# Hybrid decoder trunk: the first down block moved ahead of the second gate block in the pair stream

## The chip, the cores and the metric

One core of one Trainium2 chip. The metric is device time in microseconds (us) of one execution. Three runs of the kernel before gave 1495.41, 1496.53 and 1497.82 us, so its median is 1496.53 us. Besides TensorE (PE), VectorE (DVE), ScalarE (ACT) and GpSimd (POOL), SyncE (SP) matters here, since it issues every weight transfer.

## The reference, cut to what matters

Two layers on 256 tokens of width 1024, all in float32. Layer 0 is a state-space mixer and a dense SwiGLU, layer 1 is stick-breaking attention and a routed SwiGLU with 8 experts of width 3584, of which each token takes two. Only this last part is touched:

```python
def swiglu(h, w_gate_up, w_down):
    gate, up = jnp.split(h @ w_gate_up, 2, axis=-1)
    return (jax.nn.silu(gate) * up) @ w_down
# routed: logits -> softmax -> top 2 of 8, renormalised
for e in range(N_EXPERTS):
    out = out + gates[:, e:e+1] * swiglu(tok, w_gate_up[e], w_down[e])
```

Each expert has 1024 x 7168 gate and up weights and 3584 x 1024 down weights, 44 MB, so the eight experts are 352 MB that have to come from HBM.

## The kernel before, in words

**Weights.** Every large weight comes as a granule of 2 MB (2048 KB) into a ring of seven slots (`ring`, RING = 7). A granule has a place n in one long stream; it goes to slot n % 7. SP issues the loads strictly in the order of the stream (`load`, line 511): before load n it waits until PE has released the granule seven places earlier (semaphore `used[n % 7]`), and consumers wait on `landed[n % 7]`. One SP instruction order thus governs everything: a load whose slot is already free still stands behind an earlier load whose slot is not.

**Experts.** An expert's hidden width of 3584 is cut into seven blocks f = 0..6 of 512 columns. Each block has three granules: gate (g), up (u) and down (d). The experts are taken in four pairs: expert a with many tokens, expert b with few. A pair has 42 granules, named ag, au, ad, bg, bu, bd with the block number. `pair_order` (line 74) gives their order in the stream; `PAIR_AT` and `pair_place` turn it into places, which SP, PE, ACT and DVE all use. The first five granules of the first pair (AHEAD = 5) are loaded before the routing is known, from expert 0.

**What PE does in a pair (`pair_wide`).** In block f it takes: for the tail tokens of a (up to 32 beyond 128) the product with au f, then the main product with ag f, then bg f-1, the tail's ad f, the main product with au f, bu f-1, a turn (transposes, line 2799) of the product, the tail's ag f+1, bd f-2, and last the main product with ad f. A main product splits each operand in a rounded part and a rest and runs three passes: 24 matmuls of line 2355 for one granule. Its last matmul releases the slot. ACT rounds each half granule (line 1063, `w`, a buffer of three halves) and DVE computes the rest (line 1918, `ring_lo`); both go through the granules in the order ag, au, ad of each block. Products for b and for the tail are those of line 2667 (gate and up) and line 2679 (down); they read the ring directly. In block 0 there are no b granules yet: the order of last uses is ag0, au0, ad0, ag1, bg0, au1, bu0, ad1. Before the main product of ad0 PE makes the gather of expert b's tokens (line 2622) and the turn.

**What runs.** In this trace pairs 0 and 1 have a tail (their PE rows hold tail products), pair 2 has none, and pair 3 is the light kind (`pair_light`), in which expert a has at most 64 tokens and goes through lines 2667 and 2679 too. Between pairs stand the gather for the next pair (line 2602) and the scatter of results (lines 2649 to 2659).

**The other branch.** If the routing does not allow pairs, experts run one by one with granule numbers of their own (`gate_at`, `up_at`, `down_at`). The five preloaded granules lie where the pair stream put them, so this branch has to find them there.

Of the kernel before, what the change touches and what calls it, by code (L numbers as in the profile page):

```python
# [72 lines left out]

def pair_order():

    order = [("ag", 0), ("au", 0), ("ag", 1), ("au", 1), ("ad", 0), ("bg", 0), ("ad", 1), ("bu", 0), ("ag", 2)]
    for f in range(2, FB):
        order += [("au", f), ("bg", f - 1), ("ad", f), ("bu", f - 1)]
        if f < FB - 1:
            order += [("ag", f + 1)]  # L80
        order += [("bd", f - 2)]
    return order + [("bg", FB - 1), ("bu", FB - 1), ("bd", FB - 2), ("bd", FB - 1)]
# [30 lines left out]
def pair_place(what, f):  # L113

    return N_MOE + PAIR_AT[(what, f)]


def pair_turn(p, what, f):
# [19 lines left out]
def program(nc, x, c, ada_w, ada_b, norm_g, s5_w_in, s5_lambda_re, s5_lambda_im, s5_b_re, s5_b_im,  # L138
# [3 lines left out]
    with ctx:  # L142
# [364 lines left out]
        def _(sp):  # L507
# [77 lines left out]
                for p in range(PAIRS):  # L585
                    pair_weights(p, 0 if p else AHEAD)
            with sp.Else():
                swiglu_weights(moe_w_gate_up[0][0], moe_w_down[0][0], lambda g: N_MOE + g,
                               lambda g: (N_MOE + g) // RING, AHEAD)
                with sp.Fori(1, NE) as e:  # L590
                    expert = sp.value_load(turn_i[0:1, bass.ds(e, 1)], min_val=0, max_val=NE - 1)
                    swiglu_weights(gate_up[bass.ds(expert * D, D), :], downs[bass.ds(expert * FF, FF), :],
                                   lambda g: N_MOE + g, lambda g: e * (PER_EXPERT // RING) + (N_MOE + g) // RING)
            for tt in range(TT):
                sp.wait_ge(x_new, 7 + tt)
                sp.dma_start(out[0][P * tt:P * tt + P, :], x_sb[:, tt, :]).then_inc(out_written, 16)
# [77 lines left out]
        def _(act):  # L674
# [473 lines left out]
            with act.Else():  # L1148
                with nc.Fori(0, NE, engines=[act.engine], hint_back_edge=True) as e:
# [10 lines left out]
                    def narrow(passes):  # L1160

                        if len(passes) == 2:
                            act.wait_ge(xe1_ps, e + 1)
                            for k in range(KD):
                                ins = act.activation(xe1[:, k, :], ps[:, G_BANK + k // 4, P * (k % 4):P * (k % 4) + P],
                                                     ACT.Identity, bias=shift_col(3, k), scale=scale_c[:, 3, k:k + 1])
                            ins.then_inc(xe1_done, 1)

                        def silu_item(f, ch, width):
                            if ch:  # L1170
                                act.wait_ge(t_gate, tails + f + 1)
                                if f:
                                    act.wait_ge(m_act, e * FB + f)
                                act.activation(sg[:, 0:4 * width], ps[:, G_BANK, 0:4 * width], ACT.Silu).then_inc(t_silu, 1)
                            else:
                                wait_used(act, N_MOE + gate_at(f), moe_turn(gate_at(f)))
                                if len(passes) == 2:
                                    act.wait_ge(t_act, tails + f + 1)
                                elif f:
                                    act.wait_ge(m_act, e * FB + f)  # L1180
                                act.activation(sg[:, 0:4 * width], ps[:, G_BANK, 0:4 * width], ACT.Silu).then_inc(m_silu, 1)

                        def turned_item(f, ch, width):
                            shares = P // width
                            if ch:
                                act.wait_ge(t_tr, tails + f + 1)
                            else:
                                act.wait_ge(m_tr, e * FB + f + 1)
                            src = ps[:, T_BANK, 0:4 * width].rearrange("p (c r n) -> p r c n", r=shares, n=width)
                            dst = aT[:, ch].rearrange("p (r c) n -> p r c n", r=shares)[:, :, :, 0:width]  # L1190
                            act.activation(dst, src, ACT.Copy).then_inc(t_aT if ch else m_aT, 1)

                        for f in range(FB + 1):
                            for ch, width in passes:
                                if f < FB:
                                    silu_item(f, ch, width)
                                if f:
                                    turned_item(f - 1, ch, width)
                        gathered_out(e + 1, len(passes) == 1)
                        results_out([ch for ch, _ in passes])  # L1200

                    def whole(tail):
# [3 lines left out]
                        def w_round(h):  # L1206

                            g, half = divmod(h, 2)
                            if g in plain and not half:
                                return  # L1210
                            wait_landed(act, N_MOE + g, moe_turn(g))
                            if h >= 3:
                                before, part = divmod(h - 3, 2)
                                if part:
                                    wait_used(act, N_MOE + before, moe_turn(before))
                                else:
                                    act.wait_ge(h0_read, split * PER_EXPERT + before + 1)
                            act.activation(half3(h).bitcast(F32R), ff_half(gran(N_MOE + g), half), ACT.Copy
                                           ).then_inc(whi_done, 2 if g in plain else 1)

                        def silu_main(f):
                            wait_used(act, N_MOE + gate_at(f), moe_turn(gate_at(f)))
                            if f:
                                act.wait_ge(m_act, e * FB + f)
                            act.activation(sg[:, :], ps[:, G_BANK, :], ACT.Silu).then_inc(m_silu, 1)
# [51 lines left out]
        def _(dve):  # L1277
# [714 lines left out]
            with dve.Else():  # L1992
                with nc.Fori(0, NE, engines=[dve.engine], hint_back_edge=True) as e:
# [27 lines left out]
                    def narrow(passes):  # L2021
# [6 lines left out]
                        def product_item(f, ch, width):  # L2028
# [6 lines left out]
                                                  ALU.mult).then_inc(t_act, 1)  # L2035
                            else:
                                dve.wait_ge(m_silu, e * FB + f + 1)
                                wait_used(dve, N_MOE + up_at(f), moe_turn(up_at(f)))
                                if f:
                                    dve.wait_ge(m_tr, e * FB + f)  # L2040
                                dve.tensor_tensor(a_sb[:, 0:4 * width], sg[:, 0:4 * width], ps[:, U_BANK, 0:4 * width],
# [9 lines left out]
                    def whole(tail):  # L2051
# [6 lines left out]
                        def w_rest(h):  # L2058

                            g, half = divmod(h, 2)  # L2060
                            if g in plain and not half:
                                return
                            dve.wait_ge(whi_done, (split + 1) * (2 * PER_EXPERT) + h + 1)
                            if tail:
                                dve.wait_ge(*tail_read[g])
                            dve.tensor_tensor(ff_half(ring_lo[(N_MOE + g) % RING][:, :], half).bitcast(F32R),
                                              ff_half(gran(N_MOE + g), half), half3(h), ALU.subtract
                                              ).then_inc(wlo_done, 2 if g in plain else 1)

                        def product_main(f):  # L2070
                            dve.wait_ge(m_silu, e * FB + f + 1)
                            wait_used(dve, N_MOE + up_at(f), moe_turn(up_at(f)))
                            if f:
                                dve.wait_ge(m_tr, e * FB + f)
                            dve.tensor_tensor(a_sb, sg, ps[:, U_BANK, :], ALU.mult).then_inc(m_act, 1)
# [62 lines left out]
        def _(pe):  # L2138
# [761 lines left out]
            with pe.Else():  # L2900
                scatter(0, 1)
                with nc.Fori(0, NE, engines=[pe.engine], hint_back_edge=True) as e:
# [12 lines left out]
                    def narrow(passes):  # L2915
# [32 lines left out]
                                pe.wait_ge(done_m, e * FB + f)  # L2948

                        def gate_product(f, ch, width):  # L2950
                            n = N_MOE + gate_at(f)
                            wait_landed(pe, n, moe_turn(gate_at(f)))
                            wait_last(m_silu, t_silu, f, ch)
                            product(G_BANK, ch, gran8(n), width).then_inc(t_gate if ch else used[n % RING], 1)

                        def up_product(f, ch, width):
                            n = N_MOE + up_at(f)
                            wait_landed(pe, n, moe_turn(up_at(f)))
                            wait_last(m_act, t_act, f, ch)
                            product(U_BANK, ch, gran8(n), width).then_inc(t_up if ch else used[n % RING], 1)  # L2960
# [19 lines left out]
                            ins.then_inc(t_tr if ch else m_tr, 1)  # L2980

                        def down_product(f, ch, width):
                            n = N_MOE + down_at(f)
                            wait_landed(pe, n, moe_turn(down_at(f)))
                            if ch:
                                pe.wait_ge(t_aT, tails + f + 1)
# [27 lines left out]
                    def whole(tail):  # L3014
# [3 lines left out]

                        def tail_in(g, f, at, done):

                            n = N_MOE + g
                            wait_landed(pe, n, moe_turn(g))
                            if at == TAIL_UP:
                                pe.wait_ge(t_silu, tails + f + 1)
# [8 lines left out]

                        def tail_down(g, f):

                            n = N_MOE + g
                            wait_landed(pe, n, moe_turn(g))
                            pe.wait_ge(t_aT, tails + f + 1)
                            if f == 0:
# [9 lines left out]
                            pe.wait_ge(wlo_done, (split + 1) * (2 * PER_EXPERT) + 2 * g + half + 1)  # L3049

                        def halves(g, half, cols):
                            low = ff_half(ring_lo[(N_MOE + g) % RING][:, :], half)
                            return [w.rearrange("p (k n) -> p k n", n=cols) for w in (half3(2 * g + half), low)]

                        def main_in(g, f, bank, free):

                            n = N_MOE + g
                            if f:
                                pe.wait_ge(free, e * FB + f)
                            for half in range(2):  # L3060
# [17 lines left out]

                        def main_down(g, f):

                            n = N_MOE + g
                            pe.wait_ge(m_aT, e * FB + f + 1)
                            if f == 0:
                                pe.wait_ge(sc_done, 4 * e + 8)
# [81 lines left out]
```

## Time and profile before

| | us |
|---|---|
| median of 3 runs | 1496.53 |
| the profiled execution's own time | 1497.91 |
| its span in the trace | 1496.1 |
| PE busy | 1346.0 (90%) |
| DVE busy | 673.5 (45%) |
| ACT busy | 520.2 (35%) |
| mean granted TensorE clock | 0.966 |
| weight queue's share of the 16 DMA engines' span | 81.2% |

The page cuts the span into 40 slices of 37.4 us. The routed part begins near 596 us, when the routing result lets SP and PE go on, and fills the rest. A slice's DMA digit and its GB/s say how busy the transfers were; a slice's PE digit says the same of matmuls, with the reservation that matmuls are pipelined and their ends modelled. Where both are high in the same slices, only the waits say which of the two the other one waits for.

### The profile page before, as it was taken

How to read it: one execution, taken by the hardware profiler on the slowest of the kernel's cores; microseconds unless marked ns; L12 is line 12 of the kernel's file. 1: busy time of each engine (PE TensorE's matmuls, PEld its weight loads, DVE VectorE, ACT ScalarE, POOL GpSimd, SP SyncE). 2: the span in 40 equal slices, each digit the busy share in tenths (PEclk: the TensorE clock that was granted, in tenths of full speed). 3: DMA queues.
4: the chain of work that ended last, by engine and by line, in shares of the span. 5: the costliest groups of instructions: out<-in, count | busy, mean ns of one | idle time of the engine just before them, and what ended most of it. 6: DMA issues, size and time to landing. Idle time of an engine off the chain costs nothing.

```text
span 1496.1 us, 25369 instructions
## 1 busy us (share of the span) xinstructions
PE 1346.0 (90%) x11187; PEld 966.0 (65%) x11188; DVE 673.5 (45%) x754; ACT 520.2 (35%) x566; POOL 35.8 (2%) x66
## 2 busy tenths in 40 slices
PE   3899899999999897999999999999888889887776
PEld 2674578888789646777776777766675665443332
DVE  5953344445354526655453755443764553100002
ACT  2323433343253604444442454443553442000001
POOL 3000000000010002000000000000000000000000
PEclk8989999999999997999999999999998999999999
DMA  8874794554495214689999989999999999999994
GB/s 285 323 289 156 285 394 170 203 189 169 169 340 205 75 57 171 224 337 410 412 411 412 384 319 411 411 410 412 399 351 411 414 411 411 412 412 413 412 413 190
DMA packets 206791, 474.28 MB, mean 317 GB/s; under 512 B 9986, under 2 KB 10030, under 8 KB 206670
## 3 DMA queue, kind: packets, MB, share of 16 engines
q1 hardware_dynamic: 199968, 470.83, 81.2%
q10 hardware_dynamic: 6702, 1.71, 0.5%
q8 instruction: 92, 1.51, 0.4%
q14 instruction: 29, 0.24, 0.0%
HBM read 471.47 MB, written 1.05 MB: 316 GB/s over the span
## 4 chain that ended last, share of the span: by engine, by line
PE 64%; DMA 16%; SPq 12%; DVE 3%; ACT 2%; issue 1%; ACTq 1%; POOL 0%; POOLq 0%; DVEq 0%
PE ps L2355 39%; DMA ring<-in_moe_w_down_dram 13%; SPq L511 12%; PE ps L2667 6%; PE ps L2679 5%; DMA ring<-in_ada_w_dram 3%; PE ps L2528 2%; PE ps L2331 2%; PE ps L2166 1%; PE ps L2230 1%; PE ps L2291 1%; PE ps L2622 0%; PE ps L2659 0%; PE ps L2252 0%; PE ps L2456 0%
## 5 line engine op out<-in xcount | busy, mean ns | idle before, releaser
L1918 DVE TENSOR_TENSOR ring_lo<-ring,w 128x2048 fp32r<-128x2048 f32 x126 | 288.2, 2290 | 186.3 <-ACT w L1063 149.0
L1063 ACT ACTIVATE w<-ring 128x2048 fp32r<-128x2048 f32 x126 | 240.4, 1912 | 221.0 <-PE ps L2355 208.8
L2667 PE MATMUL ps<-ring,arena 128*32 128x128 f32 (+1 forms) x5376 | 240.2, 294 | 28.6 <-DMA ring<-in_moe_w_gate_up_dram 24.8
L2667 PEld LDWEIGHTS ps<-ring,arena 128*32 128x32 f32 (+1 forms) x5376 | 183.3, 115 | 89.2 <-DMA ring<-in_moe_w_gate_up_dram 34.8
L2355 PE MATMUL ps<-ring_lo,x_hi 128*128 128x512 f32 x592 | 231.2, 391 | 0.0
L2355 PE MATMUL ps<-w,x_hi 128*128 128x512 f32 x336 | 135.3, 403 | 4.5 <-DVE ring_lo L1918 2.6
L1541 DVE TENSOR_TENSOR ring_lo<-ring,w_hi 128x2048 fp32r<-128x2048 f32 x42 | 95.6, 2290 | 89.0 <-ACT w_hi L788 89.0
L2355 PE MATMUL ps<-w,x_lo 128*128 128x512 f32 x336 | 131.3, 391 | 0.0
L2355 PEld LDWEIGHTS ps<-ring_lo,x_hi 128*128 128x128 f32 x592 | 111.3, 188 | 21.2
L2679 PE MATMUL ps<-ring,tri 128*32 128x512 f32 (+1 forms) x448 | 72.6, 662 | 38.1 <-DMA ring<-in_moe_w_down_dram 36.1
L788 ACT ACTIVATE w_hi<-ring 128x2048 fp32r<-128x2048 f32 x42 | 78.8, 1908 | 49.1 <-PE ps L2355 42.1
L2355 PE MATMUL ps<-w_hi,x_hi 128*128 128x512 f32 x224 | 89.4, 399 | 0.0
L2355 PE MATMUL ps<-w_hi,x_lo 128*128 128x512 f32 x224 | 87.4, 390 | 0.0
L2355 PEld LDWEIGHTS ps<-w,x_hi 128*128 128x128 f32 x336 | 63.1, 188 | 32.5 <-issue 17.7
L2355 PE MATMUL ps<-w,a_hi 128*128 128x512 f32 x168 | 70.1, 417 | 3.6 <-DVE a_lo L1956 3.6
L2355 PEld LDWEIGHTS ps<-w,x_lo 128*128 128x128 f32 x336 | 63.1, 188 | 13.5
L2355 PE MATMUL ps<-ring_lo,a_hi 128*128 128x512 f32 x168 | 67.4, 401 | 0.0
L2355 PE MATMUL ps<-w,a_lo 128*128 128x512 f32 x168 | 67.1, 400 | 0.0
L2679 PEld LDWEIGHTS ps<-ring,tri 128*32 128x32 f32 (+1 forms) x448 | 17.7, 123 | 72.7 <-DMA ring<-in_moe_w_down_dram 42.6
L2166 PE MATMUL ps<-ring,c 128*32 128x512 f32 x384 | 50.3, 677 | 15.3 <-DMA ring<-in_ada_w_dram 15.3
L2679 PE MATMUL ps<-ring,arena 128*32 128x512 f32 (+1 forms) x336 | 55.0, 613 | 9.8 <-DMA ring<-in_moe_w_down_dram 8.6
L1880 DVE TENSOR_TENSOR c<-c,ps 128x128 f32<-128x128 f32 (+1 forms) x28 | 8.8, 315 | 96.2 <-PE ps L2667 96.2
(399 smaller groups left out, 1694.3 us busy)
## 6 DMA issues: line engine op xcount, KB each, us to landing
ring<-in_moe_w_gate_up_dram SPq DMA_DIRECT2D x112, 2048.0 KB, 17.5
ring<-in_moe_w_down_dram SPq DMA_DIRECT2D x56, 2048.0 KB, 18.3
ring<-in_ada_w_dram SPq DMA_DIRECT2D x24, 2048.0 KB, 11.1
ring<-in_ffn_w_gate_up_dram SPq DMA_DIRECT2D x14, 2048.0 KB, 11.6
ring<-in_ffn_w_down_dram SPq DMA_DIRECT2D x7, 2048.0 KB, 7.7
ring<-in_sb_w_qkv_dram SPq DMA_DIRECT2D x6, 2048.0 KB, 8.6
ring<-in_s_w_out_dram SPq DMA_DIRECT2D x2, 2048.0 KB, 7.7
ring<-in_sb_w_out_dram SPq DMA_DIRECT2D x2, 2048.0 KB, 14.5
```

The lines of the kernel that those rows point to most:

```text
L511: sp.dma_start(dst, src).then_inc(landed[n % RING], 16)
L788: act.activation(ff_half(w_hi[:, g % 2, :], half).bitcast(F32R), ff_half(gran(ff_place(g)), half), ACT.Copy).then_inc(whi_done, 1)
L1063: act.activation(half3(h).bitcast(F32R), ff_half(gran(pair_place(*main_granule(n))), half), ACT.Copy).then_inc(whi_done, 1)
L1541: dve.tensor_tensor(ff_half(ring_lo[(ff_place(g)) % RING][:, :], half).bitcast(F32R), w, ff_half(w_hi[:, g % 2, :], half), ALU.subtract).t ...
L1918: dve.tensor_tensor(ff_half(ring_lo[place % RING][:, :], half).bitcast(F32R), ff_half(gran(place), half), half3(h), ALU.subtract).then_inc ...
L2166: ins = pe.matmul(ps[32 * j:32 * j + 32, ada_bank(i), :], c32[:, 4 * part_k + k, :], gran8(places[r])[:, 4 * part_k + k, :], start=k == 0, ...
L2230: ins = pe.matmul(ps[:, Y_BANK + b // 2, 256 * (b % 2):256 * (b % 2) + 256], gran8(N_WIN)[:, k, P * b:P * b + P], hT[:, k, :], start=k == ...
L2331: ins = pe.matmul(ps[:, 2 * i + half, :], yT[:, k, P * tt:P * tt + P], gran4(WOUT_PLACES[half])[:, k, 512 * n:512 * n + 512], start=k == 0 ...
L2355: ins = pe.matmul(dst, stationary[a].bitcast(F32R), moving[b].bitcast(F32R), start=start and i == 0, stop=stop and i == 2)
L2528: ins = pe.matmul(ps[:, Y_BANK + 2 * tt + r, :], oT[:, k, P * tt:P * tt + P], gran8(n)[:, k, :], start=k == 0, stop=k == KD - 1)
L2667: ins = pe.matmul(dst[width * r:width * r + width, 0:cols], x[:, k, 0:width], weights[:, k, cols * r:cols * r + cols], start=k == 0, stop= ...
L2679: ins = pe.matmul(ps[width * r:width * r + width, bank, :], a[:, j, 0:width], weights[:, j, 512 * h:512 * h + 512], start=first and i == 0 ...
```

## The change

In `pair_order` the granule ad0 moves from the fifth place of each pair to the third, ahead of ag1 and au1. Nothing else of the order changes, and neither do the number of loads, their sizes or any instruction of PE, ACT, DVE or POOL in the pairs; only slot numbers of these three granules change. The second part of the diff keeps the other branch consistent: `expert_place` maps its granule numbers 2, 3 and 4 (gate 1, up 1, down 0) to the places 3, 4 and 2.

```diff
-    order = [("ag", 0), ("au", 0), ("ag", 1), ("au", 1), ("ad", 0), ("bg", 0), ("ad", 1), ("bu", 0), ("ag", 2)]
+    order = [("ag", 0), ("au", 0), ("ad", 0), ("ag", 1), ("au", 1), ("bg", 0), ("ad", 1), ("bu", 0), ("ag", 2)]
...
+def expert_place(g):
+
+    return N_MOE + {2: 3, 3: 4, 4: 2}.get(g, g)
...
-                swiglu_weights(moe_w_gate_up[0][0], moe_w_down[0][0], lambda g: N_MOE + g,
+                swiglu_weights(moe_w_gate_up[0][0], moe_w_down[0][0], lambda g: expert_place(g),
...
-                            n = N_MOE + gate_at(f)
+                            n = expert_place(gate_at(f))
```

All other lines of the diff replace `N_MOE + g` by `expert_place(g)` in the one-by-one branch.

## Rows read from the trace of the kernel before

**Rows 1.** Busy time by stretch: us, each engine, PEclk, DMA share, GB/s.
```profile
611.00:648.00 37.00, 37.00 (x420) 28.66 (x418) 21.88 (x15) 14.89 (x12) 0.00 (x0) 1.00 0.47 165
852.00:874.00 22.00, 22.00 (x274) 16.89 (x272) 11.66 (x8) 10.40 (x8) 0.00 (x0) 1.00 0.59 211
1080.00:1096.00 16.00, 16.00 (x183) 12.90 (x181) 11.37 (x6) 8.32 (x6) 0.00 (x0) 1.00 0.70 241
1096.00:1240.00 144.00, 122.66 (x1094) 90.05 (x1097) 76.94 (x48) 64.88 (x51) 0.00 (x0) 0.92 1.04 412
1240.00:1476.00 236.00, 191.16 (x1426) 103.25 (x1419) 23.25 (x56) 16.75 (x43) 0.00 (x0) 0.99 1.03 407
```
**Rows 2.** Chain of waits, pair 0: start, us, what (main products of ad0, ag1, au1).
```profile
623.12 5.66 PE ps L2355 x24
...
630.67 5.67 PE ps L2355 x24
...
640.05 5.67 PE ps L2355 x24
```
**Rows 3.** Line 511, pair 0: load ag2, then load bu2, each with its landing.
```profile
L511 SPq DMA_DIRECT2D ring<-in_moe_w_gate_up_dram x1: 373/373/373, 615.4 to 615.4; - x1
DMA to landing us min/median/max: 7.6/7.6/7.6
...
L511 SPq DMA_DIRECT2D ring<-in_moe_w_gate_up_dram x1: 373/373/373, 684.7 to 684.7; - x1
DMA to landing us min/median/max: 10.7/10.7/10.7
```
**Rows 4.** PE's waits for transfers, 736 to 770, then 959 to 1000: total, times, longest.
```profile
PE ps L2679 <- DMA ring<-in_moe_w_down_dram: 4.1, 2, 2.6
...
PE ps L2679 <- DMA ring<-in_moe_w_down_dram: 4.4, 2, 2.3
```
**Rows 5.** Chain of waits, pair 1: main products of ad0, ag1, au1.
```profile
849.08 5.66 PE ps L2355 x24
...
856.63 5.67 PE ps L2355 x24
...
866.01 5.67 PE ps L2355 x24
```
**Rows 6.** Line 511, pair 1: landing of au2 (issued 862.5); load bu2 with its landing.
```profile
DMA to landing us min/median/max: 8.7/8.7/8.7
...
L511 SPq DMA_DIRECT2D ring<-in_moe_w_gate_up_dram x1: 373/373/373, 910.7 to 910.7; - x1
DMA to landing us min/median/max: 10.9/10.9/10.9
```
**Rows 7.** Timeline, pair 2: PE ends ad0; SP issues au2 and bg1, then ad2.
```profile
1080.21 0.39 PE L2355 MATMUL ps<-w,a_lo 128*128 128x512 f32 x1
...
1086.21 7.92 SPq L511 DMA_DIRECT2D ring<-in_moe_w_gate_up_dram  x2
1094.31 0.44 SPq L511 DMA_DIRECT2D ring<-in_moe_w_down_dram  x1
```
**Rows 8.** Line 511, pair 2: load ag2 and landing; ad2's landing; load bu2 and landing.
```profile
L511 SPq DMA_DIRECT2D ring<-in_moe_w_gate_up_dram x1: 5536/5536/5536, 1067.3 to 1067.3; - x1
DMA to landing us min/median/max: 19.2/19.2/19.2
...
DMA to landing us min/median/max: 12.0/12.0/12.0
...
L511 SPq DMA_DIRECT2D ring<-in_moe_w_gate_up_dram x1: 373/373/373, 1133.6 to 1133.6; - x1
DMA to landing us min/median/max: 9.7/9.7/9.7
```
**Rows 9.** Timeline of PE: the waits for bd0 (pair 2) and for ad0 (pair 3).
```profile
1123.25 3.64 PE L2679 MATMUL ps<-ring,tri 128*32 128x512 f32 x16 [4.41 <-DMA ring<-in_moe_w_down_dram]
...
1286.82 6.43 PE L2679 MATMUL ps<-ring,arena 128*64 128x512 f32 x16 [4.98 <-DMA ring<-in_moe_w_down_dram]
```

More of the change, by code:

```diff
@@ L592, in _ @@
                     swiglu_weights(gate_up[bass.ds(expert * D, D), :], downs[bass.ds(expert * FF, FF), :],
-                                   lambda g: N_MOE + g, lambda g: e * (PER_EXPERT // RING) + (N_MOE + g) // RING)
+                                   lambda g: expert_place(g), lambda g: e * (PER_EXPERT // RING) + (N_MOE + g) // RING)
             for tt in range(TT):
@@ L1175, in silu_item @@
                             else:
-                                wait_used(act, N_MOE + gate_at(f), moe_turn(gate_at(f)))
+                                wait_used(act, expert_place(gate_at(f)), moe_turn(gate_at(f)))
                                 if len(passes) == 2:
@@ L1210, in w_round @@
                                 return
-                            wait_landed(act, N_MOE + g, moe_turn(g))
+                            wait_landed(act, expert_place(g), moe_turn(g))
                             if h >= 3:
@@ L1214, in w_round @@
                                 if part:
-                                    wait_used(act, N_MOE + before, moe_turn(before))
+                                    wait_used(act, expert_place(before), moe_turn(before))
                                 else:
                                     act.wait_ge(h0_read, split * PER_EXPERT + before + 1)
-                            act.activation(half3(h).bitcast(F32R), ff_half(gran(N_MOE + g), half), ACT.Copy
+                            act.activation(half3(h).bitcast(F32R), ff_half(gran(expert_place(g)), half), ACT.Copy
                                            ).then_inc(whi_done, 2 if g in plain else 1)
                         def silu_main(f):
-                            wait_used(act, N_MOE + gate_at(f), moe_turn(gate_at(f)))
+                            wait_used(act, expert_place(gate_at(f)), moe_turn(gate_at(f)))
                             if f:
@@ L2037, in product_item @@
                                 dve.wait_ge(m_silu, e * FB + f + 1)
-                                wait_used(dve, N_MOE + up_at(f), moe_turn(up_at(f)))
+                                wait_used(dve, expert_place(up_at(f)), moe_turn(up_at(f)))
                                 if f:
@@ L2065, in w_rest @@
                                 dve.wait_ge(*tail_read[g])
-                            dve.tensor_tensor(ff_half(ring_lo[(N_MOE + g) % RING][:, :], half).bitcast(F32R),
-                                              ff_half(gran(N_MOE + g), half), half3(h), ALU.subtract
+                            dve.tensor_tensor(ff_half(ring_lo[expert_place(g) % RING][:, :], half).bitcast(F32R),
+                                              ff_half(gran(expert_place(g)), half), half3(h), ALU.subtract
                                               ).then_inc(wlo_done, 2 if g in plain else 1)
@@ L2071, in product_main @@
                             dve.wait_ge(m_silu, e * FB + f + 1)
-                            wait_used(dve, N_MOE + up_at(f), moe_turn(up_at(f)))
+                            wait_used(dve, expert_place(up_at(f)), moe_turn(up_at(f)))
                             if f:
@@ L2956, in up_product @@
                         def up_product(f, ch, width):
-                            n = N_MOE + up_at(f)
+                            n = expert_place(up_at(f))
                             wait_landed(pe, n, moe_turn(up_at(f)))
@@ L2982, in down_product @@
                         def down_product(f, ch, width):
-                            n = N_MOE + down_at(f)
+                            n = expert_place(down_at(f))
                             wait_landed(pe, n, moe_turn(down_at(f)))
@@ L3019, in tail_in @@
                         def tail_in(g, f, at, done):
-                            n = N_MOE + g
+                            n = expert_place(g)
                             wait_landed(pe, n, moe_turn(g))
@@ L3034, in tail_down @@
                         def tail_down(g, f):
-                            n = N_MOE + g
+                            n = expert_place(g)
                             wait_landed(pe, n, moe_turn(g))
@@ L3051, in halves @@
                         def halves(g, half, cols):
-                            low = ff_half(ring_lo[(N_MOE + g) % RING][:, :], half)
+                            low = ff_half(ring_lo[expert_place(g) % RING][:, :], half)
                             return [w.rearrange("p (k n) -> p k n", n=cols) for w in (half3(2 * g + half), low)]
                         def main_in(g, f, bank, free):
-                            n = N_MOE + g
+                            n = expert_place(g)
                             if f:
@@ L3079, in main_down @@
                         def main_down(g, f):
-                            n = N_MOE + g
+                            n = expert_place(g)
                             pe.wait_ge(m_aT, e * FB + f + 1)
```

## The prediction

> **What bounds the kernel now.** I read the page first: in its slices nearly all of the routed part has PE and the transfers busy together, so a share of busy time decides nothing. The stretches [rows 1] do. While the weight stream runs without a break it shows a DMA share of 1.04 and 412 GB/s, which is 2048 KB, or 2.097 MB, in 5.1 us. Three stretches fall short of it, one near the start of each of pairs 0, 1 and 2, and PE is busy for the whole of all three. There PE computes on granules that it has and SP waits for a slot. After 1096 us there is no such gap: the stream is full to the end of pair 3, and PE waits for it: rows 9 show the first of four such waits of 4.4 to 6 us in pair 2, and one in pair 3 [rows 9]. So the end is set by the last landing plus a fixed rest, and the last landing by how much the stream has idled before 1096. A full stream has a share of 1.04, so the idle is 37 x (1 - 0.47/1.04) = 20.3 us, 22 x (1 - 0.59/1.04) = 9.5 us and 16 x (1 - 0.70/1.04) = 5.2 us [rows 1].
>
> Next I read who held the slot. SP loads in stream order, and load i needs the release of granule i-7. Seven places after the beginning of a pair come bu0, ag2, au2, bg1, ad2: before, they need ag0, au0, ag1, au1 and ad0. PE's order is ag0, au0, ad0, ag1, au1, as the chain shows [rows 2, 5]: ad0 is released first of the last three and its slot asked for last. Afterwards au2 needs ad0, bg1 needs ag1, ad2 needs au1. No engine has an instruction more, and none is moved on any queue but SP's.
>
> **The change, pair 0.** A lone load lands 7.6 us after its issue [rows 3], one behind others 5.1 us after the one before. The releases are the ends of the main products: ad0 at 628.8, ag1 at 636.3, au1 at 645.7 [rows 2]. So au2 goes out 7.6 us earlier, bg1 9.4 us earlier, and ad2 at the same 645.7, but as a lone load: it lands at 653.4. Before, bg1 and ad2 went out together there, and ad2 landed one transfer later still. That is worth 5 to 6 us at this point. It does not all last, because PE computes without a pause in these blocks and releases no faster: bu2 goes out at 684.7 when PE is done with ad2, and landed 10.7 us later, at 695.4 [rows 3]. It can't land before 684.7 + 7.6 = 692.3. The advance left is **3.1 us**. Later loads of the pair keep it.
>
> Does PE turn it into time? It waits for down blocks twice later in the pair, 4.1 us together [rows 4]. As 3.1 is less than 4.1, these waits shrink by 3.1 and the rest of the stream and PE are both earlier by 3.1.
>
> **Pair 1** repeats this on the shifted clock; I give the times of before. ad0, ag1 and au1 end at 854.7, 862.3 and 871.7 [rows 5]. ad2, lone, lands at 871.7 + 7.6 = 879.3. bu2 again decides: issued at 910.7, landed 10.9 us later at 921.6 [rows 6], now at 918.3 at the earliest: **3.3 us**. PE's waits of 4.4 us [rows 4] take it up.
>
> **Pair 2** has no tail work, and ad0 ends at 1080.6 [rows 7]; ag1 is released when the two loads of the second row begin, 1086.2; and au1 at 1093.8 (the pair of loads ends at 1094.13, the second takes 0.37). ag2 lands at 1067.3 + 19.2 = 1086.5 [rows 8]. Now au2 can follow without a gap (1091.6), bg1 too (1096.7), and ad2 lands at the later of 1101.8 and 1093.8 + 7.6 = 1101.4. It landed at 1094.3 + 12.0 = 1106.3 [rows 7, 8]. Gain 4.5 to 4.6 us, of an idle of 5.2 [rows 1]; I take **4.6**. After that the stream is full. bd0 arrives 4.6 us earlier, which is just the wait of 4.41 us before it [rows 9]. The next bu2 has 9.7 us from issue to landing [rows 8], so 2.1 us of room over a lone load, and its release follows that wait, so it moves too.
>
> **Pair 3.** The stream was full (1.03) [rows 1] and PE waited 4.98 us for ad0 [rows 9]. That wait goes: ad0 lands two transfers, 10.2 us, sooner. It is worth nothing, since PE's other work waits for loads behind a full stream: what is late next is ag1, a transfer later than before.
>
> ag1 and au1 land one transfer (5.1 us) later in each pair. I cost this at nothing in pairs 0 to 2: in pair 0 all five are there before the routing is; in pairs 1 and 2 their first readers come after the gather and the turn. If that cover were gone, each pair would pay up to 5.1 us. The five loads ahead of the routing and the one-by-one branch cost nothing here.
>
> **Sum.** 3.1 + 3.3 + 4.6 = 11.0 us. The profiled execution took 1497.91 us (span 1496.1) and would take 1486.9. It was 1.4 us above the median of the runs, 1496.53, so the median of the changed kernel should be 1485.5 us. Bounds of each term: a lone load of pair 1 took up to 8.7 us [rows 6], which would leave 2.0, 2.2 and 3.5 (ad2 at 1102.5, and a little for the load behind it), sum 7.7. At the other end, if the room at bu2 is wider than I think, PE's waits cap the first two terms at 4.1 and 4.4 [rows 4] and the idle the third at 5.2, sum 13.7. I take the middle value since 7.6 was measured for loads into an empty queue with nothing beside them.
>
> The Trainium skill, page "DMA: Bandwidth & Descriptors", section "Anatomy of one DMA — SWDGE (gpsimd) path", fits one transfer as 2.0 us plus its bytes at 436 GB/s. By that a lone load would take 6.8 us, an estimate from the page, and pairs 0 and 1 would each gain 0.8 us more, 12.6 us in all. The row says 7.6 us for this queue, so the row is used.
>
> **Rivals.**
> (a) Lone loads at the slow end: 7.7 us, 1488.8. For it, the first lone load of pair 1 had the 8.7; against it, the 7.6 of pair 0 [rows 3].
> (b) The advances of pairs 0 and 1 are lost again, because some release between bu2 and PE's first wait is late too, so that only pair 2 counts: 4.6 us, 1491.9. Against it: both stretches end with the stream full, and PE waits for it there.
> (c) More than the sum, up to the cap: 13.7 us, 1482.8.
> (d) Nothing: ag1 or au1, a transfer later, takes the place of ad0 as what PE waits for, in pairs 1 and 2, 2 x 5.1 = 10.2 us against 11.0: 1495.7. It decides where PE would ask for ag1 within 5.1 us of its old landing. Before, no PE wait for a gate or up block shows in pairs 1 and 2, and the stretch of each gap is fully busy.
> (e) Slower, by the TensorE clock. After PE's wait for bd0 in pair 2 its 16 matmuls took 3.64 us [rows 9], and the granted clock of that part of the trace is 0.92 [rows 1], so part of it runs at 1.2 and not 2.4 GHz. Once the stream is ahead, waits in pair 2 move and some grow: with the first gone, the second can be 4.4 + 2.3. If half clock then lasted through the ad, ag and au products, 5.7 us each, PE would lose 3 x 5.7 = 17.1 us a block, of which the wait covers 6.7; with four blocks 40 us lost, less 11: 1526. It decides from where half clock outlasts the wait's room of 2.1 us at bu2. For it: those 3.64 us; against it: four waits like that already stand in pair 2 and the stream stayed full.
> On this the skill's page "TensorE: Matmul & The Clock Gate" (Part 1) says that the array falls to half clock when it idles and gets the full clock back under sustained work; by that rule the slow part ends early in each block, and (e) fails. The trace agrees so far, with the stream full behind each wait.
>
> **Chances.** Forecast 0.66; (a) 0.12; (b) 0.07; (c) 0.08; (d) 0.04; (e) 0.03. The range from 1482.5 to 1490.5 takes in the forecast, (a) and (c), and about 0.85 of the chance. Within 0.2% is within 3.0 us, about what a measurement of this kernel can tell from no change. Forecast, (a), (b), (c) are all faster by more than that: 0.93; (d) is the same: 0.04; (e) slower: 0.03.
>
> **What would show it.** In the trace after: au2 issued at ad0's end and bg1 at ag1's, in pairs 0 to 2; the gap of pair 2 closed, those of pairs 0 and 1 spread and shorter; bu2 of pairs 0 and 1 landing about 7.6 us after issue; PE's waits of 4.1 and 4.4 us down to about 1 each; the wait of 4.41 us before bd0 gone, later ones of pair 2 still there; pair 3 a full stream and no wait for ad0. Pair 1 should be entered 3 us earlier, pair 2 6.4, pair 3 11. Wrong would be: PE waiting for ag1 or au1, a gap in pairs 2 or 3 that was not there, or pairs entered early without an earlier last landing.

## The result and the profile after

The changed kernel took 1485.11 us (median of 4 runs, 1484.42 to 1485.58), the kernel before, beside it, 1497.17 us. The ratio is 0.992 with a 95% interval from 0.9903 to 0.9938: 12.1 us faster by the medians, 9.3 to 14.5 by the interval. Forecast was 1485.5 us, range 1482.5 to 1490.5. The profiled execution took 1485.06 us (span 1483.2).

The same busy-time view over the stretches in which the stream had idled, and the full one behind them (columns as in [rows 1]; from 1240 to 1463 the share was 1.03):

```profile
611.00:648.00 37.00, 37.00 (x475) 28.73 (x474) 22.46 (x16) 16.26 (x14) 0.00 (x0) 1.00 0.63 220
848.00:874.00 26.00, 26.00 (x347) 20.27 (x346) 15.38 (x10) 12.02 (x12) 0.00 (x0) 1.00 0.89 334
1074.00:1096.00 22.00, 20.59 (x203) 16.59 (x202) 14.84 (x9) 12.34 (x10) 0.00 (x0) 1.00 1.02 395
1096.00:1240.00 144.00, 124.84 (x1185) 92.73 (x1184) 73.41 (x50) 61.36 (x52) 0.00 (x0) 0.93 1.04 411
```

Reckoned as in the prediction, the idle of pair 0 at this place is 37 x (1 - 0.63/1.04) = 14.6 us after 20.3, of pair 1 26 x (1 - 0.89/1.04) = 3.8 after 9.5, and of pair 2 22 x (1 - 1.02/1.04) = 0.4 after 5.2. The windows of pairs 1 and 2 are longer than before because the idle is spread. In pairs 0 and 1 part of this saving is lost again a little later, as the sections below show; in pair 2 the idle is simply gone.

The release order now shows directly. In the chain of waits of pair 0 the main products of ad0, ag1 and au1 stand as in [rows 2], and SP's timeline has the loads au2 and bg1, then ad2:

```profile
620.87 5.67 PE ps L2360 x24
...
628.42 5.67 PE ps L2360 x24
...
637.79 5.67 PE ps L2360 x24
```
```profile
626.70 7.92 SPq L516 DMA_DIRECT2D ring<-in_moe_w_gate_up_dram  x2
643.62 0.37 SPq L516 DMA_DIRECT2D ring<-in_moe_w_down_dram  x1
```

au2 goes out at 626.70, 0.2 us after ad0's end at 626.54; bg1 at 634.25 (626.70 + 7.92 - 0.37), 0.2 us after ag1's end; ad2 0.2 us after au1's. In [rows 2] the first of these had to wait for ag1.

### The profile page after: what moved, and what is told of

The parts are those of the page before. It is cut to its first block, busy times and chain, and to the rows that moved or that the text cites. A ratio compares the mean times of both kernels' runs of the same rounds, so it can differ in the third digit from the quotient of the medians.

```text
span 1483.2 us, 25369 instructions
## 1 busy us (share of the span) xinstructions
PE 1343.1 (91%) x11187; PEld 967.1 (65%) x11188; DVE 673.3 (45%) x754; ACT 520.5 (35%) x566; POOL 36.7 (2%) x66
## 4 chain that ended last, share of the span: by engine, by line
PE 67%; SPq 14%; DMA 12%; DVE 3%; ACT 2%; issue 1%; ACTq 1%; POOL 0%; POOLq 0%; DVEq 0%
PE ps L2360 41%; SPq L516 14%; DMA ring<-in_moe_w_down_dram 9%; PE ps L2672 6%; PE ps L2684 4%; DMA ring<-in_ada_w_dram 2%; PE ps L2533 2%; PE ps L2336 2%; PE ps L2171 1%; DMA ring<-in_moe_w_gate_up_dram 1%; PE ps L2235 1%; DVE ring_lo L1923 1%; PE ps L2296 1%; PE ps L2461 1%; PE ps L2627 1%
## 6 DMA issues: line engine op xcount, KB each, us to landing
ring<-in_ffn_w_gate_up_dram SPq DMA_DIRECT2D x14, 2048.0 KB, 11.7
```

## Experiments

Times scatter more than the effects that are to be told apart: beside the experiments the kernel before ran 29 times in one batch, from 1489.45 to 1498.37 us. The traces say where the scatter sits. The next table gives, from each kernel's own trace, the issue of bu0 in pair 0 (it waits for ag0's release, which the change does not move), and the routed stretch: from that issue to the last landing of the stream. For the kernel before and the one after, these are their rows, in SP's timeline and in the view of the load line:

```profile
608.34 0.37 SPq L511 DMA_DIRECT2D ring<-in_moe_w_gate_up_dram  x1
...
L511 SPq DMA_DIRECT2D ring<-in_moe_w_down_dram x1: 2301/2301/2301, 1457.5 to 1457.5; - x1
DMA to landing us min/median/max: 18.3/18.3/18.3
```
```profile
606.07 0.37 SPq L516 DMA_DIRECT2D ring<-in_moe_w_gate_up_dram  x1
...
1444.66 2.30 SPq L516 DMA_DIRECT2D ring<-in_moe_w_down_dram  x1
```

The last load of the kernel after landed 18.3 us behind its issue too. So the stretches are 1475.8 - 608.3 = 867.5 and 1463.0 - 606.1 = 856.9 us.

| kernel | bu0 issued at | routed stretch | shorter by | T expected | time against before, beside it |
|---|---|---|---|---|---|
| before | 608.3 | 867.5 | | | |
| after | 606.1 | 856.9 | 10.6 | 11.0 | 0.992 [0.9903, 0.9938] |
| full (the same again) | 605.7 | 857.0 | 10.5 | 11.0 | 0.9945 [0.9924, 0.9966] |
| only0 | 608.8 | 864.4 | 3.1 | 3.0 | 0.9983 [0.9969, 0.9997] |
| only1 | 603.3 | 864.2 | 3.3 | 3.0 | 0.9985 [0.9973, 0.9997] |
| only2 | 607.5 | 862.4 | 5.1 | 4.6 | 0.9957 [0.9941, 0.9974] |
| only3 | 607.3 | 867.8 | -0.3 | 0 | 0.9986 [0.9971, 1.0002] |
| mid | 603.4 | 858.5 | 9.0 | 8.8 | 0.9942 [0.9921, 0.9963] |
| second | 606.2 | 864.4 | 3.1 | 5.2 | 0.9981 [0.9967, 0.9995] |
| swap01 | 606.7 | 855.8 | 11.7 | 12.0 to 12.6 | 0.9926 [0.9905, 0.9946] |

The issue of bu0 lies anywhere from 603.3 to 608.8 us, with no order in it: that is scatter of what comes before the pairs.

Each stretch is read from one execution. The same kernel twice (after, full) agrees within 0.1 us, but a single reading can be off by about 1 us, since now and then a transfer of the full stream lands about 1 us late, and where that happens differs from trace to trace. In only2 it is the very last load, 19.3 us from issue to landing and not 18.3, and PE's rest behind it was as much shorter: to the end of the span only2 gained 6.0 us, the others the same as in the table within 0.4 us.

**The new order in one pair alone.** A list of heads by pair replaces the one head:

```diff
-    order = [("ag", 0), ("au", 0), ("ad", 0), ("ag", 1), ("au", 1), ("bg", 0), ("ad", 1), ("bu", 0), ("ag", 2)]
+    order = list(PAIR_HEADS[p]) + [("bg", 0), ("ad", 1), ("bu", 0), ("ag", 2)]
...
-PAIR_AT = {item: i for i, item in enumerate(pair_order())}
+PAIR_AT = [{item: i for i, item in enumerate(pair_order(p))} for p in range(PAIRS)]
```

In only2, PAIR_HEADS holds the new head ag0, au0, ad0, ag1, au1 at place 2 and the old one elsewhere; the others likewise. T, R and U are the three explanations that the next text names; the texts after it use the letters again.

> The new order in pair 0 alone, the old one in pairs 1 to 3. Theory T (what counts is the order in which SP asks for slots against the order in which PE releases them; the gain of a pair is what the first late block leaves of it): about 3.0 us faster than before, bu2 of pair 0 landing 7.6 to 8 us after its issue, pairs 1 and 2 with their old gaps. Rival R (what counts is that ad0 itself is there sooner for those who read it): no gain, since ad0 of pair 0 was there before the routing in both kernels. Rival U (an unrelated earlier start of the routed part): under 1 us or up to 2, with no change in the gaps.

Measured: 1492.81 us against 1495.45, stretch 3.1 us shorter. bu2 of pair 0, which decides the term, in the view of the load line:

```profile
L522 SPq DMA_DIRECT2D ring<-in_moe_w_gate_up_dram x1: 373/373/373, 685.2 to 685.2; - x1
DMA to landing us min/median/max: 8.0/8.0/8.0
```

It was 10.7 [rows 3]. The gap of pair 2 stayed (share 0.70 from 1080 to 1096, as in [rows 1]). T holds, and R falls: ad0 had been there before the routing in both. U falls too, since the stretch begins with the issue of bu0 and so leaves the earlier or later start out.

> The new order in pair 1 alone. T: 3.0 us faster than before (the trace of the changed kernel gave 8.2 less 5.1 us of advance in this pair), gap of pair 1 spread, those of pairs 0 and 2 as before. R: below 1 us, since PE never waited for ad0 in pair 1.

Measured: 1492.76 us against 1495.45, stretch 3.3 us shorter; bu2 of pair 1 landed 8.9 us after its issue, before 10.9 [rows 6]. PE's two waits in pair 0 were still there, 4.1 us together, since that pair had the old order.

> The new order in pair 2 alone. T: 4.6 us faster, the gap of 5.2 us closed, the wait before bd0 gone. R: 2.2 us at most, the wait for DVE before the main product of ad0, at whose head the chain of waits had the landing of ad0.

Measured: 1489.33 us against 1495.45, stretch 5.1 us shorter. Its stretch of the gap, in the view of busy time, is a full stream:

```profile
1080.00:1096.00 16.00, 14.59 (x177) 11.63 (x176) 10.73 (x8) 8.04 (x7) 0.00 (x0) 1.00 1.05 407
```

R could give 2.2 us at most and falls, whether the gain is read as 5.1 us or, to the end of the span, as 6.0.

> The new order in pair 3 alone, where PE waited 4.98 us for ad0 in the kernel before. T: no change (within 0.5 us), since the stream is full there, although that wait goes. R: up to 5 us faster, the whole of that wait.

Measured: 1494.53 us against 1495.45, the interval includes 1; stretch 0.3 us longer. The wait for ad0 is gone, in PE's timeline:

```profile
1281.51 3.65 PE L2690 MATMUL ps<-ring,arena 128*64 128x512 f32 x16 [0.52 <-issue]
```

Before it was 4.98 us and the same 16 matmuls took 6.43 [rows 9]. A wait of 5 us on the engine that is busiest was removed, and the time did not follow. This run separates T and R most sharply: all of the gain is in pairs where that wait was not.

The four add up to 3.1 + 3.3 + 5.1 - 0.3 = 11.2 us, against 10.5 and 10.6 for the whole.

**Half the move, and too much of it.** The heads of all pairs, with the full move in the line that goes (each + line is one kernel):

```diff
-    (("ag", 0), ("au", 0), ("ad", 0), ("ag", 1), ("au", 1)),
+    (("ag", 0), ("au", 0), ("ag", 1), ("ad", 0), ("au", 1)),   # mid
+    (("ag", 0), ("ad", 0), ("au", 0), ("ag", 1), ("au", 1)),   # second
```

> Half the move: ad0 goes between ag1 and au1, in all pairs. Only bg1 gains a release (ad0's instead of au1's); au2 still waits for ag1's. T: in pairs 0 and 1 nothing is lost against the full move, since bu2 limits both there (3.1 and 3.3 us); in pair 2 au2 lands at the old 1093.8, bg1 5.1 and ad2 10.1 us later, a gain of 2.4 instead of 4.6. Together 8.8 us between the start of the routed part and the last landing. R (ad0 sooner for its readers): half of the full gain everywhere, 5.5 us.

Measured: 1486.37 us against 1495.86, stretch 9.0 us shorter, 8.8 expected; half of the gain, as R had it, would be 5.5. In its trace pairs 0 and 1 lose nothing by the half move and pair 2 does. Device times alone do not show that: the median of mid lies 0.3 us below that of the full move beside it (1486.70), where T says 2.2 above. The start of the routed part, 2.3 us earlier in the trace of mid than in that of full, is as large as the difference looked for. So the ranking of the two rests on one trace of mid and two of the full move.

> The move taken too far: ad0 goes to the second place, ahead of au0, in all pairs. ag2 now waits for ad0's release instead of au0's, and au0 lands a transfer later. T: 3.1 us gained in pair 0; in pair 1 PE waits about 4 us for au0 at its first use, which eats the gain, 0.7 us lost; in pair 2 ag2 is alone and late, 2.8 us gained. Together about 5 us faster than before, 6 slower than the changed kernel. R: at least as fast as the changed kernel, since ad0 is there sooner still.

Measured: 1492.62 us against 1495.86. The direction is T's, and R falls: ad0 lands sooner than in any other kernel and the kernel is 5.9 us slower than the full move beside it. The size was off: stretch 3.1 us shorter, not 5.2. Pair 1 lost 3 us where I had 0.7 lost, because the wait for au0 cost more than itself, in PE's timeline:

```profile
824.83 3.00 PE L2678 MATMUL ps<-ring,arena 128*32 128x128 f32 x64 [4.30 <-DMA ring<-in_moe_w_gate_up_dram]
```

These 64 matmuls take 1.95 us at full clock, and the main product behind them took 6.27 instead of 5.73 us. With the 4.30 of the wait that is 5.9 us, of which the time that was won in pair 0 covers a part. I had priced the wait (4) and not what follows it.

**A version that goes further.** The rest of idle in pair 1 is at bu2, which asks for ad2's slot. In pairs 0 and 1 block 2 gets bu1 ahead of ad2:

```diff
-        order += [("au", f), ("bg", f - 1), ("ad", f), ("bu", f - 1)]
+        order += [("au", f), ("bg", f - 1)] + ([("bu", f - 1), ("ad", f)] if f == 2 and p in (0, 1) else [("ad", f), ("bu", f - 1)])
```

> The changed kernel with bu1 ahead of ad2 in pairs 0 and 1, so that bu2 asks for the slot of bu1, released long before, and only ag4 for that of ad2. T: the single late load at bu2 of pair 1 goes (6.71 us between landings there, 5.1 now), 1.3 to 1.6 us of advance in pair 1, of which PE's last wait of 1.3 us can take 1.3; in pair 0 at most 0.3. So 1 to 1.6 us faster than the changed kernel within the routed part, which times alone can hardly show. If ad2, a transfer later, makes PE wait, it is slower by up to 5 us in a pair.

Measured: 1484.40 us (1483.17 to 1484.88) beside 1486.70 (1484.87 to 1487.74) for the full move in the same batch, 2.3 us less, with hardly any overlap of the two sets of runs. The stretch is 1.2 us shorter than full's. PE's last wait of pair 1 was 1.1 us, in full 1.4, and no new wait for ad2 appeared. It is the fastest of the kernels tried, ahead of the one before and of the full move. By how much is less sure than that: each trace is one execution, and 1.2 us is what the order accounts for in it.

> The changed kernel again, beside the others on the same chip. T: 11.0 us faster than before, and the same 11 (3.1 + 3.3 + 4.6) between the start of the routed part and the last landing, while the start of the routed part itself scatters by some us from run to run, in either direction.

Measured: 1486.70 us against 1495.86, 9.2 us; together with the first comparison 12.1 and 9.2 bracket the 11.0. The stretch repeats to 0.1 us.

## Why the prediction was right, step by step

**The release order as cause.** Shown, by only0 to only3 and by the traces of mid and second: each pair's gain follows from which slot is asked for when. That ad0 lands sooner for its readers counts for nothing (only3, second).

**Pair 0, 3.1 us.** bu2, issued 2.3 us earlier than before, as all of the trace then was, landed 7.8 us after its issue:

```profile
L516 SPq DMA_DIRECT2D ring<-in_moe_w_gate_up_dram x1: 373/373/373, 682.4 to 682.4; - x1
DMA to landing us min/median/max: 7.8/7.8/7.8
...
L516 SPq DMA_DIRECT2D ring<-in_moe_w_gate_up_dram x1: 373/373/373, 905.4 to 905.4; - x1
DMA to landing us min/median/max: 9.1/9.1/9.1
```

10.7 [rows 3] less 7.8 is 2.9. only0, alone, gave 3.1. The lead is not quite steady: in the trace after it reads 1.9 us at pair 0's last load and 2.9 again at pair 1's first, as transfers that land 1 us late fall in other places.

**Pair 1, 3.3 us.** Here bu2 landed 9.1 us after its issue (second row pair above) and not 7.6, so that the step left 10.9 - 9.1 = 1.8 us at this load; rival (a), which had 8.7 there, was the nearer. The prediction set the 7.6 of pair 0 against (a), but that was one lone load of three: the next two of pair 0, au2 and bg1, took 8.4 and 9.0 us in the same trace.

only1 still gave 3.3 us in all. The rest came at the beginning of pair 2: there two transfers (ag1 and au1) took 5.9 and 5.4 us in the trace before, and 5.1 and 5.2 in the trace after; only1, mid and second gained the same 1 us at that place, only0 and only3 did not. So it goes with pair 1's new order, but what it is stays open. The term is right in size, 3.3 us, and its working only for 1.8 of them; that the two agree is luck.

**PE's waits take the advance up.** From 4.1 and 4.4 us, each of two waits [rows 4], to 1.3 and 1.3, each of one, in the same stretches:

```profile
PE ps L2684 <- DMA ring<-in_moe_w_down_dram: 1.3, 1, 1.3
```

I had said about 1 each (4.1 - 3.1, 4.4 - 3.3). Less the 2.3 us of the earlier start, PE entered pair 1 3.0 us sooner and pair 3 10.6, where I had 3 and 11. Pair 2 it entered 8.0 us sooner, not 6.4, as the gather for it shows (32 matmuls from 1032.96 before, from 1022.65 after). The 1.6 us more are the size of another loss that went: before, the second of the two waits of pair 1 had slow matmuls behind it, 1.6 us in all (last section), and that wait is gone. It is worth nothing in the total, since the stream was only 6.0 us ahead there and sets the end.

**Pair 2, 4.6 us.** ad2 landed 12.9 us earlier than in the trace before, and ag2 8.2 us, so that the gap gave 4.7. au2 and bg1 were issued well ahead of need, and ad2 with 8.7 us to its landing:

```profile
1071.77 5.81 SPq L516 DMA_DIRECT2D ring<-in_moe_w_gate_up_dram  x2
1084.75 0.37 SPq L516 DMA_DIRECT2D ring<-in_moe_w_down_dram  x1
```

In this trace the wait for bd0 went from 4.41 us [rows 9] to 0.41, and the next grew from 4.47 to 7.20 us, in PE's timeline:

```profile
1110.24 1.92 PE L2684 MATMUL ps<-ring,tri 128*32 128x512 f32 x16 [0.41 <-DMA ring<-in_moe_w_down_dram]
...
1140.64 3.64 PE L2684 MATMUL ps<-ring,tri 128*32 128x512 f32 x16 [7.20 <-DMA ring<-in_moe_w_down_dram]
```

That is the move of waits that rival (e) began with: 6.7 predicted, 7.20 found. But the 16 matmuls behind the longer wait took 3.64 us, as those behind 4.41 did [rows 9], the granted clock of the part was no lower (0.93 from 1096 to 1240, before 0.92 [rows 1]), and the stream stayed full. (e) fell at that point.

The move of these waits is not a fixed thing. In the trace of full, the same kernel, the wait for bd0 was still there, 3.85 us, and the next was 4.9:

```profile
1109.59 3.64 PE L2684 MATMUL ps<-ring,tri 128*32 128x512 f32 x16 [3.85 <-DMA ring<-in_moe_w_down_dram]
```

There PE was 3.7 us further on in pair 2 than in the trace after, because its wait for ring_lo at the first main product was 0.36 us and not 2.64. It spent most of that waiting for bd0, and the routed stretch was the same within 0.1 us. So the sign "the wait before bd0 gone" was no test of the prediction. That the stream sets the end from pair 2 on is what these two traces show once more.

**Pair 3, nothing.** Shown by only3. In the trace after, all loads of pair 3 from bg0 on landed 12.6 to 12.9 us earlier than before, the same to its end.

**ag1 and au1 a transfer later, nothing.** PE waited for neither in pairs 0 to 2; (d) fell. What such a loss costs where nothing covers it, second shows for au0: 5.9 us, the wait and the slow matmuls behind it.

**The total.** 2.9 + 3.1 + 4.7 = 10.7 against the 11.0 of the sum, and 10.6 in the stretch (3.1 is the lead of 6.0 us at bg0 of pair 2 less the 2.9). The span shrank by 12.9, of which 2.3 is the earlier start of bu0, which belongs to the scatter and not to the change: only0, with the same order up to there as the kernel after, issued bu0 0.5 us later than the kernel before, and only1, with the old order there, 5.0 us earlier. So the mechanism and the size of the gain were right, and that the median fell within 0.4 us of the forecast is partly luck: the second set of runs of the same kernel had its median at 1486.70, and the kernel before had 1495.45 and 1495.86 in its two larger sets, about 1 us below the 1496.53 from which the forecast was reckoned.

## What to carry to other kernels

Where a ring is refilled strictly in stream order, the order has to follow the releases, not only the needs: load i asks for the slot of granule i - 7, and one granule placed two steps after its release holds up every load behind it. Work out the gain as the old landing less the earliest one possible, at each load that waits for a release until the stream is full, and take the smallest that is left; then check that a wait of the consumer, further on, is there to take it up. A wait that sits behind a full stream, be it 5 us on the busiest engine, is worth nothing.

## What the runs showed of the hardware

**A lone load and the instruction queue.** A lone load of 2 MB took a time that depends on the place: bu2 of pair 0 landed 7.7 to 8.0 us after its issue in all five traces in which no full transfer lay ahead of it (after, full, only0, mid, second), and bu2 of pair 1 8.9 to 9.2 us in five (after, full, only1, mid, second). The traces hold a difference between the two. In the view of the transfers of the kernel after, from 2.5 to 6.5 us behind the issue of bu2, pair 0 has packets of the weight queue q1 alone, and pair 1 has this row too:

```profile
q8 instruction: 1, 0.02, 1.5%
```

The queue q8, which the page of the profile calls instruction, brings one packet of 16 KB every 6 to 25 us in the routed part, and each takes 0.9 to 1.5 us. In the ten traces 86 loads of expert weights went out alone or, as bu2, with at most the end of one transfer ahead. The 35 in which such a packet began 3.4 to 6.0 us after the issue took 8.6 to 9.2 us, and the 51 others 7.4 to 8.4. In the full stream it is alike: of 588 transfers with such a packet beside them 69 landed over 0.8 us later than usual, and of 935 without none. The packet stood 5.0 us behind the issue of bu2 of pair 1 in the trace before too, where the load ahead hid it. No run moved these packets, so that they are the cause is argued from this agreement and not tested.

**Short waits and the TensorE clock.** Behind a wait the matmuls of pairs 0 to 2 were slower in some places and not in others. The 16 matmuls of a down block took 1.92 us behind waits of 1.3, 2.30 and 2.63 us (after, before), 2.44 us behind one of 2.08 (pair 1 of the kernel before, from 994.22), 2.95 us behind one of 2.64 (pair 1 of only0), and 3.64 us behind waits of 3.85, 4.41 and 7.20 us. Over those 3.64 us the granted clock was 0.50, which is 1.2 GHz, over the 2.44 us it was 0.77, and over the 1.92 us behind the wait of 2.30 it was 1.00. The main product behind the wait of 2.08 us took 6.83 us and not 5.75. So a wait of 2 to 3 us cost more than itself in one place and not in another, and the 16 matmuls behind a wait of 7.20 us were no slower than those behind one of 3.85.
